# Weighing three of four PEER value rows on ScalarE and summing them by accumulating transposes

## The reference, cut to what matters

```
def block(args):                       # 128 tokens at a time, 4 such blocks
    xb, eb, gb = args                  # tokens, 8 heads x 16 expert numbers, gates
    ub = u_tab[eb]
    act = _gelu(jnp.einsum('td,thkd->thk', xb, ub)) * gb
    vb = v_tab[eb]
    return jnp.einsum('thk,thkd->td', act, vb)
```

## Time and profile before

| | us |
|---|---|
| median of 3 runs (3716.50 to 3721.61) | 3720.34 |
| the profiled execution, own time | 3724.16 |
| its span in the profile | 3722.1 |
| PE busy (71% of the span) | 2656.9 |
| DVE busy (54%) | 2023.1 |
| ACT busy (22%) | 802.5 |
| POOL busy (46%) | 1709.0 |

### The profile page before, as it was taken

How to read it: one execution, slowest core, us unless ns; L and a number is a source line. 1 busy time by engine, 2 the same in 40 slices (tenths; PEclk the granted TensorE clock), 3 DMA queues, 4 the chain that set the end, 5 groups by cost and what they waited for, 6 DMA issues and landing times.

```text
span 3722.1 us, 37057 instructions
## 1 busy us (share of the span) xinstructions
PE 2656.9 (71%) x14128; PEld 1993.3 (54%) x14128; DVE 2023.1 (54%) x4133; ACT 802.5 (22%) x1515; POOL 1709.0 (46%) x1389
## 2 busy tenths in 40 slices
PE   5521887218761577435677988888799998889999
PEld 3321444104430344212236877776799997777887
DVE  6599867987788977586435434454310104531010
ACT  2100121011110011111123323333231322434231
POOL 0155556665666656466732321212364643126463
PEclk8765999659985699767989978998899999999999
DMA  5398889997999989999951200000233331013332
GB/s 176 123 335 310 297 283 342 367 353 236 339 346 363 323 285 322 357 362 351 370 197 52 68 7 1 1 1 1 57 91 91 91 86 57 18 46 85 96 91 79
DMA packets 417970, 693.79 MB, mean 186 GB/s; under 512 B 35784, under 2 KB 280691, under 8 KB 417667
## 3 DMA queue, kind: packets, MB, share of 16 engines
q0 software_dynamic: 147456, 536.94, 39.4%
q1 hardware_dynamic: 270339, 154.50, 14.3%
HBM read 689.26 MB, written 2.10 MB: 186 GB/s over the span
## 4 chain that ended last, share of the span: by engine, by line
PE 50%; DVE 25%; DMA 8%; issue 5%; POOL 5%; ACT 4%; another core or an unknown queue 4%; SPq 1%; ACTq 0%; DVEq 0%; POOLq 0%
PE PS L1604 26%; DVE ring L1311 9%; PE PS L777 5%; POOL ring L610 4%; DMA ring<-in_peer_v,eidx 4%; PE PS L756 3%; DMA ring<-in_peer_u,eidx 2%; PE PS L1505 1%; DVE X L1326 1%; PE PS L1514 1%; PE PS L662 1%; PE PS L1511 1%; DVE W L1185 1%; PE PS L1614 1%
## 5 line engine op out<-in xcount | busy, mean ns | idle before, releaser
L610 POOL DMA_INDIRECT ring<-in_peer_v,eidx x512 | 584.2, 1141 | 353.9 <-PE PS L777 186.1
L610 POOL DMA_INDIRECT ring<-in_peer_u,eidx x512 | 483.8, 945 | 484.9 <-DVE eidx L1288 188.1
L1604 PE MATMUL PS<-held_uH,GW 128*128 128x264 f32 (+1 forms) x3008 | 668.9, 316 | 35.5 <-POOL BIG_value L2131 31.4
L2117 POOL TENSOR_TENSOR GW<-held_wr,GW 128x1024 fp32r<-128x1024 f32 x178 | 428.8, 2410 | 450.2 <-ACT GW L1894 450.2
L1311 DVE CUSTOM_DVE_ANT_0 ring<-ring,PS 128x1024 f32<-128x1024 f32 x512 | 603.3, 1217 | 41.0 <-DMA ring<-in_peer_u,eidx 22.4
L777 PE MATMUL PS<-ring,dg 128*128 128x512 f32 x1024 | 509.4, 636 | 133.4 <-DMA ring<-in_peer_v,eidx 115.9
L1604 PEld LDWEIGHTS PS<-held_uH,GW 128*128 128x128 f32 x3008 | 504.7, 193 | 80.0 <-issue 34.1
L1604 PE MATMUL PS<-BIG_value,GW 128*128 128x264 f32 (+1 forms) x1504 | 448.3, 313 | 0.0
L777 PEld LDWEIGHTS PS<-ring,dg 128*128 128x128 f32 x1024 | 190.6, 199 | 405.3 <-issue 203.9
L1326 DVE SCALAR_TENSOR_TENSOR X<-ring,gact,X 128x1024 f32<-128x1024 f32 x256 | 328.2, 1282 | 132.8 <-DMA ring<-in_peer_v,eidx 117.6
L1604 PE MATMUL PS<-hid,GW 128*128 128x264 f32 (+1 forms) x2304 | 368.6, 322 | 0.0
(11 more groups left out here) (463 smaller groups left out, 3585.0 us busy)
## 6 DMA issues: line engine op xcount, KB each, us to landing
held_wr<-in_w_ff SPq DMA_DIRECT2D x128, 512.0 KB, 4.1
wqr<-in_peer_wq SPq DMA_DIRECT2D x64, 512.0 KB
held_wr<-in_w_in_ab SPq DMA_DIRECT2D x18, 512.0 KB, 3.8
ring<-in_peer_u,eidx POOLq DMA_INDIRECT x512
ring<-in_peer_v,eidx POOLq DMA_INDIRECT x512
BIG<-in_w_in SPq DMA_DIRECT2D x4, 1536.0 KB, 11.3
held_wr<-in_w_qkv_c SPq DMA_DIRECT2D x12, 512.0 KB, 3.9
w_out<-in_w_out SPq DMA_DIRECT2D x1, 4096.0 KB, 19.8
```

The source lines that it names most:

```text
L610: e.indirect_dma_start(out=ring[:, i % RING, :], out_offset=None, in_=rows_u if k < HK else rows_v, in_offset=bass.IndirectOffsetOnAxis(ap ...
L1604: ins = e.matmul(bank[b + a][:, 0:w], (hi, lo)[w_][:, k * P:(k + 1) * P], (x_hi, x_lo)[x_][:, c0:c0 + w], start=(first and w_ == 0 and x_ ...
L2117: e.tensor_tensor(r(wL[i % NS]), wr[:, i % NW].rearrange("p k n -> p (k n)"), wH[i % NS], ALU.subtract).then_inc(*up(w_lo))
```

## The change

`SUMMED` now lists the expert slots with k % 4 not 0, three of four, and `ADDED` the rest. An ADDED row goes to VectorE as before. A SUMMED row is first multiplied by its weight in its ring slot by ScalarE (one instruction on 128 x 1024, in place, after waiting for the row's gather), and then PE runs eight 128 x 128 transposes of it that accumulate in banks 6 and 7, so that the banks hold the sum of the weighed rows, each piece of 128 columns transposed. The diagonals are gone. At the end of a block ScalarE copies both banks to `W4[:, 0, :]`, PE transposes the eight pieces back into the banks, and VectorE adds them to X as before. One semaphore of another part (`v_tab`) is replaced by one that is raised right behind it.

```diff
-NDG = 3
+SUMMED = [[k for k in range(HK) if k % 4] for blk in range(NB)]
+ADDED = [[k for k in range(HK) if k not in SUMMED[blk]] for blk in range(NB)]
...
     def expert_sum(e, n, blk, k):
-        if k % 2:
-            i = k // 2
-            e.wait_ge(*row_there(256 * blk + HK + k))
-            e.wait_ge(e_dg, 64 * blk + i + 1)
-            for c in range(2):
-                ins = e.matmul(bank[6 + c], dg[:, i % NDG, :], ring[:, (256 * blk + HK + k) % RING, 512 * c:512 * c + 512],
-                               start=(k == 1), stop=(k == HK - 1))
+        if k in SUMMED[blk]:
+            i = SUMMED[blk].index(k)
+            row = ring[:, (256 * blk + HK + k) % RING, :]
+            e.wait_ge(e_scaled, SUMMED_BEFORE[blk] + i + 1)
+            for j in range(8):
+                ins = e.matmul(bank[6 + j // 4][:, j % 4 * P:(j % 4 + 1) * P], row[:, j * P:(j + 1) * P], ident,
+                               start=(i == 0 and j % 4 == 0), stop=(i == len(SUMMED[blk]) - 1 and j % 4 == 3),
+                               is_transpose=True)
             ins.then_inc(*n.up(e_pv))
+    def turn_sums(e, n, blk):
+        e.wait_ge(e_sum, 2 * blk + 1)
+        turn(e, bank[6], W4[:, 0, :])
+        turn(e, bank[7], W4[:, 0, :], at=4).then_inc(*n.up(e_sum))
...
-    def diagonal(e, n, blk, i):
-        if i < 64:
-            if i >= NDG:
-                e.wait_ge(e_pv, 64 * blk + i - NDG + 1)
-            e.mul(dg[:, i % NDG, :], ident, gact[:, 2 * i + 1:2 * i + 2]).then_inc(*n.up(e_dg))
+    def scale_row(e, n, blk, k):
+        if k in SUMMED[blk]:
+            i = 256 * blk + HK + k
+            row = ring[:, i % RING, :]
+            e.wait_ge(*row_there(i))
+            e.mul(row, row, gact[:, k:k + 1]).then_inc(*n.up(e_scaled))
+    def keep_sums(e, n, blk):
+        e.wait_ge(e_pv, SUMMED_BEFORE[blk] + len(SUMMED[blk]))
+        e.copy(W4[:, 0, 0:512], bank[6])
+        e.copy(W4[:, 0, 512:1024], bank[7]).then_inc(*n.up(e_sum))
...
     def expert_add(e, n, blk, k):
-        if k % 2 == 0:
+        if k in ADDED[blk]:
...
     def experts_done(e, n, blk):
-        e.wait_ge(e_pv, 64 * (blk + 1))
         e.wait_ge(*n.now(e_ax))
+        e.wait_ge(e_sum, 2 * blk + 2)
```

More of the change, by code:

```diff
@@ L127 @@
 NAT = 6
+SUMMED = [[k for k in range(HK) if k % 4] for blk in range(NB)]
+ADDED = [[k for k in range(HK) if k not in SUMMED[blk]] for blk in range(NB)]
+SUMMED_BEFORE = [sum(map(len, SUMMED[:blk])) for blk in range(NB)]
+ADDED_BEFORE = [sum(map(len, ADDED[:blk])) for blk in range(NB)]
 FRONT_STEPS = 76
@@ L268, in emit @@
     gact = sbuf(st, "gact", [P, HK])
-    dg = sbuf(st, "dg", [P, NDG, P])
     st.close()
@@ L343, in emit @@
         "hs", "hTp", "hT", "q", "qT", "sc", "top", "idx", "ts", "gexp", "gate"))
-    e_hn, e_dot, e_gelu, e_gact, e_dg, e_pv, e_ax, e_x = (sem("e_" + x) for x in (
-        "hn", "dot", "gelu", "gact", "dg", "pv", "ax", "x"))
+    e_hn, e_dot, e_gelu, e_gact, e_scaled, e_pv, e_sum, e_ax, e_x = (sem("e_" + x) for x in (
+        "hn", "dot", "gelu", "gact", "scaled", "pv", "sum", "ax", "x"))
     t_xTp, t_xT, t_pTp, t_pT, t_pp, t_g, t_sig, t_gp, t_x, t_xn, t_hTp, t_hT, t_met = (sem("t_" + x) for x in (
@@ L499, in emit @@
     n_sq, n_sum, n_u, n_hi, lo_v, lo_g = (sem("n_" + x) for x in ("sq", "sum", "u", "high", "low_v", "low_g"))
-    v_tab, n_w16 = sem("v_tab"), sem("w16_low")
+    n_w16 = sem("w16_low")
     c_raw, c_acc, c_silu, w_raw, z_silu = (sem(x) for x in ("c_raw", "c_acc", "c_silu", "w_raw", "z_silu"))
@@ L597, in slot_free @@
             e.wait_ge(e_dot, HK * blk + k + 1)
-        elif k % 2:
-            e.wait_ge(e_pv, 64 * blk + (k - HK) // 2 + 1)
+        elif k - HK in SUMMED[blk]:
+            e.wait_ge(e_pv, SUMMED_BEFORE[blk] + SUMMED[blk].index(k - HK) + 1)
         else:
-            e.wait_ge(e_ax, 64 * blk + (k - HK) // 2 + 1)
+            e.wait_ge(e_ax, ADDED_BEFORE[blk] + ADDED[blk].index(k - HK) + 1)
     def first_pool(e):
@@ L838, in first_tensor @@
                 expert_sum(e, n, *name[1:])
+            elif name[0] == "end":
+                turn_sums(e, n, name[1])
             elif name[0] == "second":
@@ L957, in weigh_scalar @@
         e.wait_ge(e_gact, blk + 1)
-        for i in range(NDG - 1):
-            diagonal(e, n, blk, i)
     def meta_scalar(e, n):
@@ L1008, in first_scalar @@
             elif name[0] == "v":
-                if name[2] % 2:
-                    diagonal(e, n, name[1], name[2] // 2 + NDG - 1)
+                scale_row(e, n, *name[1:])
+            elif name[0] == "end":
+                keep_sums(e, n, name[1])
             elif name[0] == "second":
@@ L1319, in expert_add @@
     def expert_add(e, n, blk, k):
-        if k % 2 == 0:
+        if k in ADDED[blk]:
             i = 256 * blk + HK + k
             e.wait_ge(*row_there(i))
-            if k:
+            if k != ADDED[blk][0]:
                 e.wait_ge(*n.now(e_ax))
@@ L1949, in second_scalar @@
             squared(lambda: e.activation(sq[k % 2], hT[:, k, :], ACT.Square))
-        e.activation(bc[:, 24:32], bc[:, 0:8], ACT.Exp).then_inc(*up(v_tab))
+        e.activation(bc[:, 24:32], bc[:, 0:8], ACT.Exp)
         w16f = w16[:, :, :].rearrange("p k n -> p (k n)")
@@ L2412, in second_vector @@
         e.wait_ge(*now(dve))
-        e.wait_ge(v_tab, 1)
+        e.wait_ge(n_w16, 1)
         for w, c in rate_rows:
```

## The result

The changed kernel is slower: 3757.99 us (median of 4 runs, 3755.30 to 3760.86) against 3720.98 beside it, a ratio of 1.0103 (95% interval 1.0084 to 1.0122), some 37 us. Measured again in another session it was 1.0110 (1.0073 to 1.0148). I had forecast 3704 us, with a range of 3684 to 3752.

What follows compares the result with a forecast made beforehand. Gathers were taken to bound U steps, heads and block 3; VectorE, with PE next, the scan rounds; PE the middle and first steps. Terms -26 - 6 + 4 + 12 = -16 us from 3720.3 gave 3704 us, range 3684 to 3752.

Steps and rivals of the forecast that it cites:

- term 3: In the 24 router heads, ScalarE's scaling lengthens each slot's hold, mostly covered by queued gathers: +4 us, bounds 0 and +36.
- term 2: In middle and first steps of three blocks, PE's rows get shorter, less waits for scaling: -6 us, bounds -15 and +9.
- Term 1: In twelve scan rounds of blocks 0 to 2, two of four VectorE adds go: -26 us, bounds -31 and -13.
- Term 4: At the end of all four blocks, copies and transposes back lengthen the path: +12 us, bounds +8 and +18.
- B: At the router heads, slots are held longer and gathers run dry: slower, 3745 to 3770 us, chance 18%.
- A: V rows run at 1.2 GHz in scan rounds and heads, PE becomes the bound: slower, 3813 to 3873 us, chance 7%.
- The forecast of a clock between 0.7 and 0.9: In most of the V stages, PE's granted clock falls to between 0.7 and 0.9 under transposes.
- C: Scan rounds shorten little, VectorE waiting for rows or L721: no change, 3716 to 3722 us, chance 20%.
- D: Transposes in PSUM do not sum as the change says; same instruction durations, no time or chance of its own.

Runs made afterwards that it cites:

- beside run: Changed kernel with ScalarE doing three 128 x 342 multiplications into a scrap buffer per SUMMED row, PE taking landed rows directly: 3671.99 us, 1.0012 of the kernel before.

## Why the prediction was wrong

**The steps that failed are term 3 and term 2**, and for one reason: ScalarE's pass between a row's landing and its use was taken as covered. Term 3 said "With the gathers queued this costs nothing" and put +4 us. Its reason was the share of 1.01 in the heads, read as "No faster engine helps there". The heads grew by 26.0 us with their ends: 0.8 us a head from query to query, and 2 us before each block's first query. Block 3, for which no term but its end was given, grew by 9.6. Terms 3 and 4 together had +16 for these stages, and 35.6 were measured. The bound of +36 held for the heads; the value taken in it was wrong. The numbers for the right reading lay in the earlier trace rows: a query of 3.73 us, a POOL wait of 2.26 and a gather of 5.81 us follow one another, and the head's 16.75 us add up from such pieces. Scaling enters that loop twice, at 1.05 us, where 0.71 of scores had stood, and at 1.16; in the head shown a longer gather and rows at the lower clock came on top. The Trainium skill ("Perfetto Trace Analysis", "Identifying the Most-Contended Engine") says to judge DMA by HBM utilization and not by occupancy, which misleads with 16 engines. The trace agrees: 349 GB/s in the heads stood beside 382 in the U steps at nearly the same share.

**Term 2** was of the wrong sign: -6 us forecast, +7.3 in the middle and +12.8 in the first steps (11.0 of them in block 0), to which it had given a gain of 1 us. By size, 26 us, it is the larger miss. PE's shorter rows are real: without scaling the middle is 76.1 and the scan part 206.6. "At two places in the middle something waits for it" was seen, but not that PE's projection would stand behind rows that ScalarE scales late, and that at the lower clock two of them take 3.3 to 3.7 us. That the diagonals' waits go was true, and worth less than the new ones.

**Term 1** was nearly right (rounds of 13.0 to 14.1 us forecast; 13.38 and 14.39 shown above). From the first scan to the last the time fell by 6.0, 5.6 and 6.4 us in blocks 0 to 2, and from there to the middle by 3.7 in all: -21.7 us where -26 was forecast. Twelve rounds was a little too many, since block 2's first scan lies 11.4 us ahead of the gate product, in the U steps. That the scan part as a whole gave only -8.9 is the first steps' loss.

**Term 4** was right where it was worked out. ScalarE's last query copy to VectorE's add took 2.89 us (638.70 to 641.59) and now takes 4.96, +2.07 for +2.1, in the timelines of ScalarE, PE and VectorE of the changed kernel (below). In block 3 it was too small: from the last landing on the chain to the add it was 2.1 us before and is 8.2, with three rows behind that landing, 4.6 us of PE at a partly lower clock.

```profile
652.95 0.37 ACT L945 COPY W<-PS 128x256 f32<-128x256 f32 x1 [6.31 <-PE PS L758]
```
```profile
654.42 1.10 PE L779 MATMUL PS<-C,ring 128*128 128x128 f32 x8 [0.34 <-ACT ring L964]
656.68 1.09 PE L625 MATMUL PS<-C,W 128*128 128x128 f32 x8 [1.16 <-ACT W L970]
```
```profile
657.91 1.28 DVE L1350 TENSOR_TENSOR X<-X,PS 128x512 f32<-128x512 f32 x2 [10.84 <-PE PS L625]
```

**The rivals.** B, at 18%, named the mechanism of the heads: the slots were held longer, and the share fell to 0.96. Its point of decision, a POOL wait past about 4.5 us, was reached in block 0 by four of eight waits (5.83, 4.95, 5.65 and 5.33). That the time fell into its 3745 to 3770 is in part luck: it had +36 to +60 in the heads, where 16 were measured between queries and 26 in all, and nothing in the first steps, the middle and, beyond its end, block 3. A fell: with the scaling left out and the same transposes the kernel is faster than before, and PE was busy 109 of 148 us in block 0's heads and 114 of 170 in block 3's window. But its lower clock is there in part: rows of 1.84 us, 0.23 a transpose, stand in the chain of a head and in block 0's first steps, beside rows of 1.1. The forecast of a clock between 0.7 and 0.9 was right in the heads and in block 3 (0.86). C was right about the scan part's sum and wrong about the rounds, which got shorter by nearly what term 1 said. D fell too: the sums of transposes came out right. The Trainium skill's rule that a transpose does not count as PE work ("TensorE: Matmul & The Clock Gate", Part 4, which gives its figures for bf16) is not what these windows show for fp32: 691 of PE's 699 records in block 3's window are transposes, and the clock there was 0.86.

**What stays open.** How the cost divides between the slot's loop and ScalarE's list order, since the beside run's work was longer than the scaling and rows behind front steps were not tested alone; what the lower clock adds to the loop; and why block 0's first steps and block 3 lost as much with half of the rows.

## What to carry to other kernels

A DMA share near 1 did not tell a stage bound by its buffers' loop (1.01 at 349 GB/s) from a saturated one (0.99 at 382), so it does not say that slower release is free. Before lengthening the time a buffer is held, add up the loop that ends with its reuse (land, work, release, issue, land), read the rate beside stages known to be saturated, and try one buffer fewer: if that costs, added work in the loop will cost too. Weights that can be prepared beside the loop, as a diagonal, were worth more here than a shorter instruction behind the landing, above all when the engine that would do it works through a list in which other steps must not be late.

## What the runs showed of the hardware

- fp32 transposes with accumulation in PSUM gave the right sums; 32 in a row took 3.72 us, so 0.89 us for a 128 x 1024 row at the upper clock, and 1.84 at the lower in the chains above.
- In block 3 the granted clock was 0.86 with three of four rows as transposes and 0.57 with every second one, while identity matmuls held 1.00 there (1780 to 1880), as matmuls did before the change (0.99).
- ScalarE took 0.294 us for 128 x 1, 0.581 for 128 x 342 and 1.145 for 128 x 1024, so splitting a row into three costs half as much again.
- The same gathers took 546 to 552 us of U steps in two sessions and 580 to 591 in the others, a larger difference (38 us) than the change made.
